# A chunked gated-linear-attention scan: exponentials by a bias column on ScalarE, key products on VectorE instead of GpSimd

## What is computed

```python
def body(s, inp):
    qc, kc, vc, gc = inp
    cum = jnp.cumsum(gc, axis=-2)
    last = cum[..., -1:, :]
    s_new = (jnp.exp(last)[..., 0, :, None] * s
             + jnp.einsum('bhcd,bhce->bhde', kc * jnp.exp(last - cum), vc))
    if not with_out:
        return s_new, None
    ref = cum[..., GLA_CHUNK // 2:GLA_CHUNK // 2 + 1, :]
    att = jnp.einsum('bhid,bhjd->bhij', qc * jnp.exp(cum - ref), kc * jnp.exp(ref - cum))
    att = jnp.where(mask, att, 0.0)
    o = (jnp.einsum('bhij,bhje->bhie', att, vc)
         + jnp.einsum('bhid,bhde->bhie', qc * jnp.exp(cum), s))
    return s_new, o
```

## Time and profile before

| | us |
|---|---|
| median of 3 runs (3152.57 to 3154.92) | 3154.49 |
| profiled execution | 3149.33 |
| its span | 3147.6 |
| PE busy | 2527.1 (80%) |
| VectorE busy | 2021.6 (64%) |
| ScalarE busy | 1387.7 (44%) |
| GpSimd busy | 389.5 (12%) |

### The profile page before, as it was taken

The page is one execution under the profiler, slowest core; times in us unless marked ns, Lnnn a source line. Parts: engine busy times, 40 slices in busy tenths (PEclk is TensorE's granted clock), DMA queues, the critical chain, the costliest instruction groups (busy, mean ns, idle before and its releaser), DMA issues. The chain is left out here.

```text
span 3147.6 us, 40465 instructions
## 1 busy us (share of the span) xinstructions
PE 2527.1 (80%) x13248; PEld 2038.8 (65%) x13248; DVE 2021.6 (64%) x1922; ACT 1387.7 (44%) x1430; POOL 389.5 (12%) x411
## 2 busy tenths in 40 slices
PE   4487871794899999999816998968595799999970
PEld 0466761683788888888714886756484688888860
DVE  1569999665757677688163002348575688888855
ACT  0310011551656666677232113334331577777752
POOL 0000000000000000100060000045200100100104
PEclk8589986896899999999957999989897899999985
DMA  9344432221988887999383211014551999999956
GB/s 301 113 162 161 135 135 70 104 104 49 344 288 322 320 315 289 338 384 358 136 301 113 74 47 51 14 69 141 197 192 58 328 384 385 391 384 395 395 217 226
DMA packets 294788, 691.73 MB, mean 220 GB/s; under 512 B 22612, under 2 KB 49396, under 8 KB 294670
## 3 DMA queue, kind: packets, MB, share of 16 engines
q1 hardware_dynamic: 262722, 584.28, 51.4%
q0 software_dynamic: 17472, 56.72, 5.3%
q10 hardware_dynamic: 14496, 49.42, 4.2%
HBM read 600.34 MB, written 91.06 MB: 220 GB/s over the span
## 5 line engine op out<-in xcount | busy, mean ns | idle before, releaser
L1479 DVE TENSOR_TENSOR moe_w_lo<-moe_w_raw,moe_w_hi 128x2048 fp32r<-128x2048 f32 x384 | 862.0, 2287 | 81.5 <-ACT moe_w_hi L1408 46.5
L1408 ACT ACTIVATE moe_w_hi<-moe_w_raw 128x2048 fp32r<-128x2048 f32 x384 | 713.9, 1909 | 59.9 <-issue 38.7
L99 PE MATMUL moe_pg<-moe_w_hi,moe_xt_hi 128*128 128x512 f32 x592 | 243.1, 411 | 11.3 <-DVE moe_xt_lo L1490 5.9
L99 PE MATMUL moe_py<-moe_w_hi,moe_at_hi 128*128 128x512 f32 x592 | 242.1, 409 | 12.2 <-DVE moe_w_lo L1479 8.5
L100 PE MATMUL moe_pg<-moe_w_lo,moe_xt_hi 128*128 128x512 f32 x592 | 235.8, 398 | 0.0
L101 PE MATMUL moe_pg<-moe_w_hi,moe_xt_lo 128*128 128x512 f32 x592 | 235.5, 398 | 0.0
L100 PE MATMUL moe_py<-moe_w_lo,moe_at_hi 128*128 128x512 f32 x592 | 235.3, 397 | 0.0
L101 PE MATMUL moe_py<-moe_w_hi,moe_at_lo 128*128 128x512 f32 x592 | 235.1, 397 | 0.0
L101 PE MATMUL moe_pu<-moe_w_hi,moe_xt_lo 128*128 128x512 f32 x592 | 234.4, 396 | 0.0
L99 PE MATMUL moe_pu<-moe_w_hi,moe_xt_hi 128*128 128x512 f32 x592 | 234.1, 396 | 0.0
L100 PE MATMUL moe_pu<-moe_w_lo,moe_xt_hi 128*128 128x512 f32 x592 | 234.1, 396 | 0.0
(11 more groups left out here) (334 smaller groups left out, 5432.3 us busy)
## 6 DMA issues: line engine op xcount, KB each, us to landing
moe_w_raw<-in_moe_w SPq DMA_DIRECT2D x384, 1024.0 KB, 10.1
taps_ada_w<-in_ada_w SPq DMA_DIRECT2D x40, 1024.0 KB, 7.0
scratch_experts_out<-moe_y ACTq DMA_DIRECT2D x57, 512.0 KB, 6.5
taps_raw<-in_conv_pw_w SPq DMA_DIRECT2D x20, 512.0 KB, 8.6
scan_v<-scratch_gla_values SPq DMA_DIRECT2D x20, 512.0 KB, 4.0
comb_x<-scratch_residual SPq DMA_DIRECT2D x18, 512.0 KB, 5.4
ada_w<-in_ada_w SPq DMA_DIRECT2D x4, 2048.0 KB, 31.6
glav_raw<-in_gla_w_in SPq DMA_DIRECT2D x4, 2048.0 KB, 7.9
```

What stands on the lines that cost most here:

```text
L99: pe.matmul(out, xh, wh, start=start, stop=False)
L1408: act.activation(hi[m][:, cut, :], raw[m][p][:, cut, :], ACT.Copy).then_inc(s(f"{m}_hi{h}"), 1)
L1479: dve.tensor_tensor(lo[m][:, cut, :], raw[m][p][:, cut, :], hi[m][:, cut, :].bitcast(F32), ALU.subtract).then_inc(s(f"{m}_lo{h}"), 1)
```

## The change

The tile `cl` and its subtraction on GpSimd are gone. ScalarE makes `el` directly from `cum` as exp(-1 x `cum` + end), the end being a column of `cum` given as the bias. Since a bias is one column for one instruction, each head and chunk has an instruction of its own, 16 of 128x64 for a step where two of 128x512 stood; all 16 stand ahead of the other exponentials. `kx` and the far half of `ks` go to VectorE, in a function `keys` ahead of each `queries`. The near half of `ks` goes to ScalarE, in `near_keys`: four copies of 128x64, each with a column of `es` as scale, one such group behind each direction's `out`. GpSimd keeps the memsets and `fall`. The semaphore `ks{r}` becomes `ks_far{r}` and `ks_near{r}`.

```diff
@@ gpsimd
                 for n in range(SCAN_STEPS):
...
                     for r in range(2):
-                        cv = chunks(cum[:, r, :, tokens(r, n)])
-                        if n:
-                            pool.wait_ge(s(f"el{r}"), n)
-                        pool.tensor_tensor(chunks(cl[r][:, :, :]),
-                                           cv[:, :, :, LAST[r]:LAST[r] + 1].to_broadcast(WHOLE), cv,
-                                           ALU.subtract).then_inc(s(f"cl{r}"), 1)
...
-                        pool.tensor_tensor(kx[r][:, :, :], k[:, :, near[r]], el[r][:, :, near[r]], ALU.mult)\
-                            .then_inc(s(f"kx{r}"), 1)
...
-                        pool.tensor_tensor(ks[r][:, :, far[r]], k[:, :, far[r]], el[r][:, :, far[r]], ALU.mult)\
-                            .then_inc(s(f"ks{r}"), 1)
                         pool.wait_ge(s(f"es{r}"), n + 1)
-                        pool.wait_ge(s(f"kx{r}"), n + 1)
-                        pool.tensor_tensor(ks[r][:, :, near[r]], kx[r][:, :, :],
-                                           es[r][b][:, :, far_end[r]:far_end[r] + 1].to_broadcast(HALF_TILE),
-                                           ALU.mult).then_inc(s(f"ks{r}"), 1)
@@ tensor, turn(n)
-                        pe.wait_ge(s(f"ks{r}"), 2 * n + 2)
+                        pe.wait_ge(s(f"ks_far{r}"), n + 1)
+                        pe.wait_ge(s(f"ks_near{r}"), n + 1)
@@ scalar, exponentials(n)
                     for r in range(2):
-                        act.wait_ge(s(f"cl{r}"), n + 1)
                         if n:
-                            act.wait_ge(s(f"ks{r}"), 2 * n)
-                        act.activation(el[r][:, :, :], cl[r][:, :, :], ACT.Exp).then_inc(s(f"el{r}"), 1)
+                            act.wait_ge(s(f"ks_far{r}"), n)
+                        t0 = scan_tile(r, n) * P
+                        for h in range(HEADS):
+                            for c in range(2):
+                                at = slice(c * CHUNK, (c + 1) * CHUNK)
+                                end = t0 + c * CHUNK + LAST[r]
+                                last = act.activation(el[r][:, h, at], cum[:, r, h, t0 + c * CHUNK:t0 + (c + 1) * CHUNK],
+                                                      ACT.Exp, bias=cum[:, r, h, end:end + 1], scale=-1.0)
+                        last.then_inc(s(f"el{r}"), 1)
+                    for r in range(2):
@@ scalar
+                def near_keys(n, r):
+                    b = n % 2
+                    act.wait_ge(s(f"kx{r}"), n + 1)
+                    if n:
+                        act.wait_ge(s(f"turned{r}"), n)
+                    act.wait_ge(s(f"es{r}"), n + 1)
+                    for h in range(HEADS):
+                        last = act.activation(ks[r][:, h, near[r]], kx[r][:, h, :], ACT.Copy,
+                                              scale=es[r][b][:, h, far_end[r]:far_end[r] + 1])
+                    last.then_inc(s(f"ks_near{r}"), 1)
...
                 exponentials(0)
+                for r in range(2):
+                    near_keys(0, r)
                 turned_keys(0)
                 exponentials(1)
+                for r in range(2):
+                    near_keys(1, r)
...
                     if n + 2 < SCAN_STEPS:
                         exponentials(n + 2)
-                    out(n)
+                    for r in range(2):
+                        out(n, r)
+                        if n + 2 < SCAN_STEPS:
+                            near_keys(n + 2, r)
@@ vector
+                def keys(n, r):
+                    m = n - FIRST_LAT
+                    k = qk[:, HEADS:2 * HEADS, tokens(r, n)]
+                    dve.wait_ge(s(f"el{r}"), n + 1)
+                    if m > 0:
+                        dve.wait_ge(s("crossed"), m)
+                    if n:
+                        dve.wait_ge(s(f"ks_near{r}"), n)
+                    dve.tensor_tensor(kx[r][:, :, :], k[:, :, near[r]], el[r][:, :, near[r]], ALU.mult)\
+                        .then_inc(s(f"kx{r}"), 1)
+                    if n:
+                        dve.wait_ge(s(f"turned{r}"), n)
+                    dve.tensor_tensor(ks[r][:, :, far[r]], k[:, :, far[r]], el[r][:, :, far[r]], ALU.mult)\
+                        .then_inc(s(f"ks_far{r}"), 1)
...
                     for r in range(2):
                         decay(n, r)
                         if n + 2 < SCAN_STEPS:
+                            keys(n + 2, r)
                             queries(n + 2, r)
```

More of the change, by code:

```diff
@@ L2035, in gla_scan @@
         v = four("v", [P, HEADS * DV])
-        cl, el, cr, eq, ek, qi, ki, ks = (two(m, [P, HEADS, P]) for m in
-                                          ("cl", "el", "cr", "eq", "ek", "qi", "ki", "ks"))
+        el, cr, eq, ek, qi, ki, ks = (two(m, [P, HEADS, P]) for m in ("el", "cr", "eq", "ek", "qi", "ki", "ks"))
         kx, qx = (two(m, [P, HEADS, CHUNK]) for m in ("kx", "qx"))
@@ L2107, in _ @@
                 for n in range(SCAN_STEPS):
-                    b, m = n % 2, n - FIRST_LAT
+                    b = n % 2
                     for r in range(2):
-                        cv = chunks(cum[:, r, :, tokens(r, n)])
-                        if n:
-                            pool.wait_ge(s(f"el{r}"), n)
-                        pool.tensor_tensor(chunks(cl[r][:, :, :]),
-                                           cv[:, :, :, LAST[r]:LAST[r] + 1].to_broadcast(WHOLE), cv,
-                                           ALU.subtract).then_inc(s(f"cl{r}"), 1)
[L2116 to L2120, removed]
-                        pool.tensor_tensor(kx[r][:, :, :], k[:, :, near[r]], el[r][:, :, near[r]], ALU.mult)\
-                            .then_inc(s(f"kx{r}"), 1)
-                        if n:
-                            pool.wait_ge(s(f"turned{r}"), n)
-                        pool.tensor_tensor(ks[r][:, :, far[r]], k[:, :, far[r]], el[r][:, :, far[r]], ALU.mult)\
-                            .then_inc(s(f"ks{r}"), 1)
                         pool.wait_ge(s(f"es{r}"), n + 1)
-                        pool.wait_ge(s(f"kx{r}"), n + 1)
-                        pool.tensor_tensor(ks[r][:, :, near[r]], kx[r][:, :, :],
-                                           es[r][b][:, :, far_end[r]:far_end[r] + 1].to_broadcast(HALF_TILE),
-                                           ALU.mult).then_inc(s(f"ks{r}"), 1)
                         if n >= 2:
@@ L2258, in join, with out @@
                             .then_inc(s(f"joined{r}"), 1)
-                def out(n):
+                def near_keys(n, r):
+                    b = n % 2
+                    act.wait_ge(s(f"kx{r}"), n + 1)
[6 more added lines that the diff above has]
+                    last.then_inc(s(f"ks_near{r}"), 1)
+                def out(n, r):
                     m = n - FIRST_LAT
@@ L2263, in out @@
                         return
-                    for r in range(2):
-                        act.wait_ge(s(f"o_summed{r}"), m + 1)
-                        if m:
-                            act.wait_ge(s(f"o_out{r}"), 16 * m)
-                        act.activation(o[r][:, :], po[:, :, :].rearrange("p h n -> p (h n)"), ACT.Copy)\
-                            .then_inc(s(f"o_ready{r}"), 1)
+                    act.wait_ge(s(f"o_summed{r}"), m + 1)
+                    if m:
+                        act.wait_ge(s(f"o_out{r}"), 16 * m)
+                    act.activation(o[r][:, :], po[:, :, :].rearrange("p h n -> p (h n)"), ACT.Copy)\
+                        .then_inc(s(f"o_ready{r}"), 1)
                 exponentials(0)
+                for r in range(2):
+                    near_keys(0, r)
                 turned_keys(0)
                 exponentials(1)
+                for r in range(2):
+                    near_keys(1, r)
                 for n in range(SCAN_STEPS):
@@ L2355, in _ @@
                     for r in range(2):
+                        keys(n, r)
                         queries(n, r)
```

## The result

The changed kernel takes 3183.44 us, the median of four runs (3182.12 to 3183.71), against 3153.69 for the kernel before (3152.57 to 3154.92, four runs). The ratio is 1.0093, 95% interval 1.008 to 1.0106: **29.8 us slower**. Forecast were 3169.3 (14.8 us over 3154.5, the median then known for the kernel before) and a range of 3160 to 3181; direction and place were right, the size was half of what came, and the time lies 2.4 us above the range. The profiled execution took 3183.67 us with a span of 3181.9; against that of before (3147.6, itself 4 us under its median) the span is 34.3 us longer. Of these 34.3, 34.1 lie in the scan, from one table load of ScalarE to the next phase's: 2077.54 to 2251.09 before, 2078.16 to 2285.78 after.

A forecast was written before the change was run, and what follows sets the result against it. A chain across engines through ScalarE's exponentials, not one full engine, bounds the scan. Six loops of 19.56 us add 14.4 and the start 0.4, +14.8 on 3154.5, giving 3169.3 us; range 3160 to 3181.

The forecast's parts named there:

- The chain and its place: Six scan loops: a chain across engines through ScalarE's exponentials, the copy scan_o, PE and VectorE sets their length; +14.4 us.
- ScalarE leg, +1.65 (8.58): From the joins to scan_o in each loop: 8.58 us in place of 6.93, +1.65.
- two terms, +2.64 and -0.87: ScalarE, each loop: 16 short exponentials replace two long ones, +2.64 us; the wait for cr goes, -0.87.
- 3.7 us by which the other exponentials start later: ScalarE, each loop: the other exponentials start 3.7 us later, so cr is done by then.
- From the copy to PE, +0: From scan_o to PE's first product of the second direction: stays 1.15 us a loop.
- PE leg, 4.70 kept: PE's second-direction products until VectorE's state starts: stays 4.70 us a loop.
- the mechanism as a rival: Six loops: PE's clock falls behind longer waits, 0.6 and up to 2.4 us a loop, middle +9, 3178 us; 17%.
- Last leg, +0.26 (5.13): From VectorE's state to the next join: 5.13 us in place of 4.87, with +0.68 for the second key pair.
- Near halves at nothing: ScalarE, four instructions behind each scan_o: 0.92 us twice a loop, hidden in ScalarE's waiting, so costed at nothing.
- slack, not gain: VectorE in the loops: its work falls from 14.3 to about 12 us a loop without shortening the chain.
- The rival that VectorE is the bound: Six loops: VectorE's relief is the gain, -2.3 us a loop, -14 us, 3140 us; 8%.
- Start and tail, +0.4: Scan outside the six loops: first join -0.5 us, next loop +0.9, tail 0; together +0.4.

The follow-up runs named there:

- after_out_early: Changed kernel with the first direction's copy of po right behind the 16 short exponentials, ahead of the six long ones; 3153.4 us.
- fill_fit: Changed kernel with unread PE products in both gaps, 7 ahead of the wait for the copy of po, 4 ahead of that for qi; 3168.0 us.
- before_copy_late: Kernel before plus three unread 128x600 exponentials on ScalarE ahead of the copy of po in the six loops; 3173.3 us.
- keys_only: Changed kernel with cl back on GpSimd and two long exponentials for el; keys stay on VectorE, near halves on ScalarE; 3161.4 us.
- after: The changed kernel itself, with the whole change made to the kernel before; 3183.4 us, ratio 1.0093.
- el_only: Kernel before with only cl removed and the sixteen short exponentials for el; key products and near halves stay on GpSimd; 3175.3 us.

## Why the prediction was wrong

- **The chain and its place.** Right. The added exponentials stand ahead of the copy, PE waits for the copy, and 34.1 of 34.3 us lie in the scan. Moving one copy takes it all back (after_out_early, 3153.4).
- **ScalarE leg, +1.65 (8.58).** Nearly right: 8.96 to 9.34. The price of a short instruction was 0.238 where I took 0.23, 0.13 a loop; fill_fit has 8.71. The rest, 2.4 us in six loops, is turned keys that a slow PE delivers later. The prediction's two terms, +2.64 and -0.87, are +1.77 and not the +1.65 of its leg; fill_fit measured +1.78. Its 3.7 us by which the other exponentials start later should be 3.2 (3.68 - 0.52), which changes nothing.
- **From the copy to PE, +0.** Right, 1.15.
- **PE leg, 4.70 kept.** Here the prediction failed. It measured 6.2 to 7.6, +10.9 in six loops. The sum kept these products at their full-clock price behind a longer wait. I had named the mechanism as a rival, seen that PE's wait would grow from 1.9 to 3.6 us, given it 17% and priced it at +1.5 a loop. It came in every loop, at +1.8 a loop in this leg alone. The wait itself was 2.58 to 3.43 us, less than I took, since the first direction's products are slow too in some loops (2.72 us for a group of 1.89). In the last leg the clock cost 2.9 more and behind the turned keys 2.4. fill_fit puts the total at 15.4 us of the 29.8 (13.5 against the kernel before on each chip); before_copy_late shows it without any of the change's own instructions.
- **Why I gave it so little.** I took the clock of 1.00 in the six loops as a property of those loops. It hung on PE's gaps, which my own sum lengthened. The row for the fall was at hand, with PE idle for at least 2 us ahead of it (4.58 in the timeline), and so was a price at the slower clock; the leg behind a longer wait should have been priced with it from the start. With the rival's bounds of 0.6 and 2.4 a loop added together, 3.0, the sum would have been 3169 + 18 = 3187.
- **Last leg, +0.26 (5.13).** Right for the work: 5.11 in three of the six loops and in all loops of fill_fit. The other three had 6.07 to 6.13 by the clock.
- **Near halves at nothing.** Right. The second group waited 1.97 us for `kx` and was done before the join; the kernel with keys and near halves alone and no collision is at 3149.7.
- **VectorE.** Right: 72.56/6 = 12.1 us a loop (12.0 forecast) and slack, not gain. The rival that VectorE is the bound falls: it lost 13.5 us of work in the six loops and the time rose.
- **Start and tail, +0.4.** Too low: +0.3 to the first join (31.53 to 31.84 from the table load, forecast -0.5), +1.3 in the loop after (15.57 for 14.23, forecast +0.9), +0.5 in the tail (forecast 0), together +2.1.
- **The range** had its upper end at the clock "with some cost on top". A 17% case with bounds up to +18 us asked for 3187.

## What to carry to other kernels

Where a step is put ahead of something that PE waits for, price not only the wait but the products behind it: read what the same products took at the lower clock, and put that price into the range as soon as the new wait is longer than any after which the trace shows the full clock. An engine's busy share says little when a hand-written order puts work that nobody needs yet ahead of the one copy that frees a buffer: moving a 1 us copy of `po` was worth 30 us in one kernel and 9 in the other (6 in its six loops). When work shifts in time, look at what it now runs beside: GpSimd's `cl` cost 12 us more beside `qi` and `ki` than beside `qs` (3161.4 against 3149.7).

## What the runs showed of the hardware

- A VectorE product of 128x512 on two SBUF inputs takes 0.68 us alone and 1.52 where it starts behind a GpSimd subtraction on SBUF (keys_only, 2194.32 behind 2194.08). Where the product starts first, it keeps its 0.69 and the subtraction takes 1.48 us in place of 1.22 (the kernel before, `ki` at 2189.87 and `cl` at 2189.98). That fits the page "SBUF — State Buffer" of the Trainium skill (SBUF: two separate sides), by which the one that starts first has the shared port for its whole instruction.
- PE's granted clock went from 1.00 to 0.50 about 1 us into the new work after a wait of 3.43 us (after, work from 2181.74), but already inside a wait of 3.70 us (el_only) and of 2.65 us (after, low from about 2203.5, work from 2203.73). In most loops it came back some 3 us later; two loops of before_copy_late and the first of the changed kernel had nearly 7 us of it. After 1.91 us in the six loops of the kernel before it did not fall, nor after the one wait of 2.72 us in before_copy_late. After 2.35 us it did so in some loops and not in others of the same kernel, which gave loops of 22.8 and 21.6 us in turn. No run here gives one length of wait as the border.
- Work that nobody reads can pay: 11 products a loop, some 4.8 us of PE time, made the changed kernel 15.4 us faster.
